# Modulation in quarters, tokens turned by a diagonal product, and a rebuilt path from row sums to routing in a one-layer mixture-of-experts kernel

## What is computed

```python
mod = silu(c) @ w_mod + b_mod            # shift, scale, gate of both halves of the layer
u   = rmsnorm(x, g1) * (1 + scale1) + shift1      # latent tokens; context tokens likewise with c_ctx
xr  = u @ w_in[:, :1024]                 # first projection, both token sets
h   = forward and backward gated recurrence over conv(xr)      # LRU, 4 heads x 2 directions
m   = sigmoid(.) * ((h * gelu(.)) @ w_rnn_proj) + sigmoid(.) * (pool_mixer(.) @ w_pool_proj)
x   = x + gate1 * rmsnorm(m @ w_out, g2)
v   = rmsnorm(x, g3) * (1 + scale2) + shift2
logits = v @ router_w + router_b         # 32 experts, the best 4 of each token, softmax over the 4
for e in range(32):
    z = v @ w1[e] + b1[e]                # 1024 -> 2048
    act = min(z0, 7) * sigmoid(1.702 * min(z0, 7)) * (clip(z1, -7, 7) + 1)
    out += comb[:, e] * (act @ w2[e] + b2[e])
x   = x + gate2 * rmsnorm(out, g4)
```

## Time and profile before

| | us |
|---|---|
| median of 3 runs | 1285.29 |
| lowest and highest run | 1284.62, 1285.57 |
| the profiled execution, device time | 1285.82 |
| its span, first to last instruction | 1283.8 |
| PE busy | 1234.7 (96%) |
| DVE, ACT, POOL busy | 361.8, 221.1, 43.9 |
| moved by DMA | 476.54 MB, mean 371 GB/s |

### The profile page before, as it was taken

How to read it: one execution, slowest core, us unless ns; L and a number is a source line. 1 busy time by engine, 2 the same in 40 slices (tenths; PEclk the granted TensorE clock), 3 DMA queues, 4 the chain that set the end, 5 groups by cost and what they waited for, 6 DMA issues and landing times.

```text
span 1283.8 us, 13953 instructions
## 1 busy us (share of the span) xinstructions
PE 1234.7 (96%) x5726; PEld 560.1 (44%) x5726; DVE 361.8 (28%) x641; ACT 221.1 (17%) x373; POOL 43.9 (3%) x90
## 2 busy tenths in 40 slices
PE   6999999999999999998999999999999899999997
PEld 4445688888443333332333333333333333333333
DVE  4567787342361112111111121112111111211113
ACT  3166631110231001010000110101110000110011
POOL 2000000240000000000000000000000000000000
PEclk9999999999999999999899999999999999999999
DMA  9732568997399999999999999999999999999995
GB/s 352 266 126 86 193 218 308 346 386 281 124 395 418 426 428 432 430 430 428 429 429 434 429 426 428 420 429 426 429 428 429 430 431 432 430 431 430 423 422 211
DMA packets 70350, 476.54 MB, mean 371 GB/s; under 512 B 6736, under 2 KB 38672, under 8 KB 48048
## 3 DMA queue, kind: packets, MB, share of 16 engines
q1 hardware_dynamic: 64320, 454.23, 85.8%
q0 software_dynamic: 3456, 21.24, 4.5%
q10 hardware_dynamic: 2512, 0.21, 0.1%
HBM read 474.60 MB, written 1.05 MB: 370 GB/s over the span
## 4 chain that ended last, share of the span: by engine, by line
PE 70%; DMA 20%; ACT 4%; DVE 4%; issue 1%; ACTq 0%; DVEq 0%; SPq 0%
PE bank L975 26%; DMA arena<-in_exp_w 20%; PE bank L992 13%; PE bank L814 11%; PE bank L1037 4%; PE bank L917 3%; PE bank L734 2%; PE bank L672 2%; PE bank L927 1%; PE bank L1084 1%; PE bank L750 1%; PE bank L700 1%; ACT arena L1195 1%; ACT arena L1189 1%; ACT arena L1197 1%
## 5 line engine op out<-in xcount | busy, mean ns | idle before, releaser
L975 PE MATMUL bank<-arena,temps 128*64 128x512 f32 x2112 | 473.0, 604 | 26.3 <-DMA arena<-in_exp_w 26.3
L975 PEld LDWEIGHTS bank<-arena,temps 128*64 128x64 f32 x2112 | 152.0, 139 | 328.6 <-issue 280.9
L992 PE MATMUL bank<-arena,vtokb 128*64 128x512 f32 x1024 | 226.8, 595 | 0.1
L1759 DVE TENSOR_SCALAR vtokb<-bank 128x512 f32<-128x512 f32 x33 | 22.8, 691 | 671.5 <-PE bank L975 671.5
L992 PEld LDWEIGHTS bank<-arena,vtokb 128*64 128x64 f32 x1024 | 70.6, 137 | 133.5 <-issue 128.0
L814 PE MATMUL bank<-arena 128*128 128x256 f32 x512 | 111.2, 379 | 0.0
L1304 ACT ACTIVATE vtokb<-vtokb 128x512 f32<-128x512 f32 x33 | 20.8, 629 | 504.5 <-DVE vtokb L1759 504.5
L814 PEld LDWEIGHTS bank<-arena 128*128 128x128 f32 x512 | 97.3, 190 | 14.9 <-issue 1.9
L1037 PE MATMUL bank<-vtokb,hot 64*128 64x512 f32 x256 | 65.4, 630 | 0.0
L750 PE MATMUL bank<-arena 128*128 128x512 f32 x128 | 56.3, 593 | 0.4 <-ACT arena L1190 0.4
L1319 ACT ACTIVATE vtokb<-bank 128x512 f32<-128x512 f32 x32 | 19.1, 598 | 204.1 <-PE bank L992 204.1
(11 more groups left out here) (286 smaller groups left out, 881.4 us busy)
## 6 DMA issues: line engine op xcount, KB each, us to landing
arena<-in_exp_w SPq DMA_DIRECT2D x115, 2048.0 KB, 22.8
arena<-in_exp_w SPq DMA_DIRECT2D x36, 4096.0 KB, 31.5
arena<-in_w_in SPq DMA_DIRECT2D x20, 1024.0 KB, 6.6
arena<-in_w_mod POOLq DMA_DIRECT2D x16, 1024.0 KB, 7.7
arena<-in_w_mod SPq DMA_DIRECT2D x16, 512.0 KB, 11.3
arena<-in_exp_w SPq DMA_DIRECT2D x6, 1024.0 KB, 22.0
arena<-in_w_pool_proj SPq DMA_DIRECT2D x4, 1024.0 KB, 14.1
arena<-in_w_rnn_proj SPq DMA_DIRECT2D x4, 1024.0 KB, 10.3
```

The lines of the kernel that those rows point to most:

```text
L975: done = mm(psum[4 + q][h * SLOTS:(h + 1) * SLOTS, :], xg[:, kx // 4, kx % 4, :], w1_at[s][:, r, o:o + HALF], start=False, stop=(k == KT - 1))
L992: last = mm(psum[6][h * SLOTS:(h + 1) * SLOTS, :], actT[:, c, r, :], w2_at[s][:, r, h * HALF:(h + 1) * HALF], start=(c == 0 and r == 0), s ...
L1759: v.tensor_scalar(glu, psum[4][:, :], LIMIT, None, ALU.min).then_inc(glu_ready, 1)
```

## The change

- *Tokens.* DVE no longer scales the tokens. It scales four copies of the identity by the tokens' inverse roots (`scaler`, 128x128), and PE multiplies each block of tokens with the diagonal: an ordinary product with 128 columns in place of a transpose.
- *Modulation.* `w_mod` comes in four quarters of 256 channels, two transfers of four rows for each operand (1 KB pieces instead of 2 KB). `mod_columns(g)` gives each channel block k a column group of its own (k mod 4) and 512 columns; the four partial sums are added by `turn_mod(g)`, which multiplies the copied rows with `fold`, a matrix of two columns. The first projection runs in quarters: for g = 0 to 2 all four j with k = 2g and 2g+1, with the next quarter's `mod_columns` ahead of j = 2 and its `turn_mod` inside j = 3; then j = 0 to 3 with k = 6 and 7. The first gates wait for all four quarters.
- *Row sums.* Two jobs in place of six. Each writes up to four sums side by side in column groups of 32, without the copy to all partitions; ACT copies them once and issues 24 transfers of 32x512 values that spread them. DVE makes the rows after the second pool projection has been read, not before the first.
- *Second token block.* Half of the scale product is made ahead (`scaled_parts`), the transposes start from that, DVE takes over one copy, the values are made in two halves behind the routing. `fill` products and the sums of the last gate's row (`sum_g2`) stand elsewhere.
- *Routing.* The mask comes from a replace-and-compare of the four best instead of indices and one-hot; the weights are made from all 32 exponentials.
- *Table and last chunks.* The table is turned ahead of the last part of item 0's first map. The last item's chunk 2 is loaded in two parts, chunk 3 in two instead of three.

```diff
-                    v.tensor_scalar(xin[:, t, :], xin[:, t, :], stat[:, 8 + t:9 + t], None, ALU.mult).then_inc(tok_scaled, 1)
+                    v.tensor_scalar(scaler[t], ident[:, :], stat[:, 8 + t:9 + t], None, ALU.mult).then_inc(tok_scaled, 1)
...
-                        last = nc.tensor.transpose(b[:, j * P:(j + 1) * P], xin[:, t, k * P:(k + 1) * P], ident[:, :])
+                        last = mm(b[:, j * P:(j + 1) * P], xin[:, t, k * P:(k + 1) * P], scaler[t], start=True, stop=True)
...
             def mod_columns(g):
...
-                    for q in range(2):
-                        for w in range(2):
-                            c = 32 * (2 * q + w)
...
-                            last = mm(psum[2 * g][c:c + 32, 0:256], sT[:, 32 * k:32 * k + 32], cols_q,
-                                      start=(k == 0), stop=(k == KT - 1))
...
+                    c = 32 * (k % 4)
+                    last = mm(psum[g % 2 * 2][c:c + 32, :], sT[:, 32 * k:32 * k + 32], modw[g][:, k, :, :],
+                              start=(k < 4), stop=(k >= 4))
...
             def turn_mod(g):
...
-                for j in range(2):
-                    last = nc.tensor.transpose(psum[2 * g + 1][:, j * P:(j + 1) * P], modrow[g][:, j * P:(j + 1) * P], ident[:, :])
+                for n in range(4):
+                    last = mm(psum[g % 2 * 2 + 1][:, 2 * n:2 * n + 2], modrow[g][:, n * P:(n + 1) * P], fold[:, :], start=True, stop=True)
...
+                    for g in range(3):
+                        for j in range(4):
+                            if j == 2:
+                                mod_columns(g + 1)
+                            if j == 3:
+                                xr_rows(j, 2 * g)
+                                turn_mod(g + 1)
+                            else:
+                                xr_rows(j, 2 * g)
+                            last = xr_rows(j, 2 * g + 1)
...
-                    end_job(mm(b[:, :], ones[:, :], acc[n // 4][:, n % 4 * HALF:(n % 4 + 1) * HALF], start=True, stop=True))
+                    for q in range(2 * len(ACC_ROWS[n])):
+                        last = mm(b[32 * q:32 * q + 32, :], ones[:, 0:32], acc[n][:, q * HALF:(q + 1) * HALF], start=True, stop=True)
...
+                        for to in range(0, P, 32):
+                            act.dma_start(row[g][to:to + 32, half * HALF:(half + 1) * HALF],
+                                          rowsum[n][p:p + 32, :]).then_inc(sums_landed, 16)
...
                 elif kind == "rk":
-                    fill(b, FILL[2] - 1)
                     sum_g2(1)
+                    fill(b, 2)
...
-                link(v.max_index(ixu[:, 8 * t:8 * t + 8], mx[:, t, :], lg[:, t, :]))
...
+                link(v.match_replace(lgr[:, t, :], mx[:, t, :], lg[:, t, :], NEVER))
+                v.tensor_tensor(mask[:, t, :], lgr[:, t, :], lg[:, t, :], ALU.not_equal).then_inc(mask_ready, 1)
```

More of the change, by code:

```diff
@@ L32 @@
 MORE = 16
-FILL = (3, 1, 2)
+NEVER = 3.0e38
 CPI = 6
@@ L85, in front_plan @@
     plan += [("pw", g, "A") for g in range(4)]
-    plan += [("rs", n, "A") for n in range(6)]
+    plan += [("rs", n, "A") for n in range(2)]
     plan += [("pp", c, "V") for c in range(4)]
@@ L758, in _ @@
                     mod_columns(0)
+                    pe.wait_ge(consts_ready, 2)
+                    fill(psum[3], 1)
                     turn_mod(0)
-                    fill(psum[3], 1)
+                    fill(psum[3], 1, 256)
                     arrive("xr", 0)
@@ L850, in _ @@
                         k = 4 * q + j
-                        last = nc.tensor.transpose(b[:, j * P:(j + 1) * P], mG[:, t, k * P:(k + 1) * P], ident[:, :])
+                        last = nc.tensor.transpose(b[:, j * P:(j + 1) * P], mG[:, 0, k * P:(k + 1) * P], ident[:, :])
                     end_job(last)
@@ L959, in first_map @@
                         pe.wait_ge(xg_ready, 2)
+                    if first and c == 3:
+                        turn_table()
                     s = slot_of(i, c)
@@ L1153, in _ @@
             a.activation(lamw[:, 16:32], lamw[:, 0:16], ACT.Exp, scale=-1.0).then_inc(lam_exp, 1)
-            for g in range(2):
+            for g in range(4):
                 act.wait_ge(mod_ready, g + 1)
@@ L1157, in _ @@
                 act.wait_ge(read_dve, read_at[number["xt", 3]][1])
-                for k in range(4 * g + 1, 4 * g + 4, 2):
+                for k in (2 * g + 1,):
                     for s in range(2):
@@ L1228, in _ @@
                 ins.then_inc(read_act, 1)
-            for n in range(6):
+            for n in range(2):
                 b = job_of("rs", n)
-                r = row[ACC_ROWS[n // 4][n % 4 // 2]]
-                a.activation(r[:, n % 2 * HALF:(n % 2 + 1) * HALF], b[:, :], ACT.Copy).then_inc(read_act, 1)
+                used = 64 * len(ACC_ROWS[n])
+                a.activation(rowsum[n][0:used, :], b[0:used, :], ACT.Copy).then_inc(read_act, 1)
+                act.wait_ge(read_act, read_at[number["rs", n]][1])
+                for m, g in enumerate(ACC_ROWS[n]):
+                    for half in range(2):
+                        p = 32 * (2 * m + half)
+                        for to in range(0, P, 32):
+                            act.dma_start(row[g][to:to + 32, half * HALF:(half + 1) * HALF],
+                                          rowsum[n][p:p + 32, :]).then_inc(sums_landed, 16)
             a.activation(stat[:, 16:18], ones[:, 0:2], ACT.Sqrt).then_inc(act_warm, 1)
@@ L1425, in take_mod @@
                 dve.wait_ge(read_dve, read_at[number["xt", 3]][1])
-                for k in range(4 * g, 4 * g + 4, 2):
+                for k in (2 * g,):
                     for s in range(2):
@@ L1615, in tokens_of, with residual, variance_of_sum @@
                 link(v.reciprocal(stat[:, 18 + t:19 + t], stat[:, 16 + t:17 + t]))
+            def residual(t, h):
                 dve.wait_ge(xres_landed, 16)
+                r = slice(h * HALF, (h + 1) * HALF)
+                v.scalar_tensor_tensor(x1[:, t, r], mG[:, t, r], stat[:, 18 + t:19 + t], x1[:, t, r],
+                                       ALU.mult, ALU.add).then_inc(x1_ready, 1)
+            def variance_of_sum(t):
+                dve.wait_ge(ssq3_ready, 2 * t + 2)
+                s0, s1 = (small[:, 68 + 2 * t + q:69 + 2 * t + q] for q in range(2))
+                link(v.tensor_tensor(stat[:, 20 + t:21 + t], s0, s1, ALU.add))
+                v.tensor_scalar(stat[:, 22 + t:23 + t], stat[:, 20 + t:21 + t], 1.0 / D, EPS, ALU.mult, ALU.add).then_inc(var3, 1)
@@ L1673, in _ @@
             for t in range(TT):
[L1674 to L1680 removed]
+                ins = v.scalar_tensor_tensor(comb_v[:, t, :], ex[:, t, :], small[:, 48 + t:49 + t], mask[:, t, :], ALU.mult, ALU.mult)
+            ins.then_inc(comb_ready, 1)
             dve.wait_ge(comb_ready, 1)
```

272 lines of the change are left out of this document (148 added, 124 removed).

## The result

The changed kernel takes 1300.35 us (median of 4, 1298.41 to 1301.97) against 1285.43 for the kernel before on the same chip: ratio 1.0116, 95% interval 1.0103 to 1.0129. That is 14.9 us slower, where 2.2 were forecast, and outside the range. The profiled execution took 1299.69 us with a span of 1298.0, 14.2 more than before; I work with that difference.

The account below looks back on a forecast made before the run. PE was taken to bound the kernel up to its last output projection, then the expert weight stream. 7.0 - 3.4 - 1.1 - 0.3 = +2.2 us gave 1287.5 against 1285.29, range 1283.5 to 1291.0.

Parts of the forecast that it names:

- cost 0: Spreading the row sums by 24 transfers: cover of 3 to 7 us before PE's small product, so no added time.
- second part: Row sums: two jobs of 0.86 us replace 5.14 us on PE, minus 3.4 us, with nothing waiting in their place.
- What bounds the kernel: PE up to its last output projection at 347.5 us, each microsecond moving the end by one; then the expert weight stream.
- Start of the projection: First projection after tokens and first modulation quarter: starts at 23.3 us, 1.3 earlier than before (bounds 22.5 and 24.5).
- The factor of the diagonal product: Token blocks: a diagonal product costs twice a transpose, 0.22 against 0.13 us at the fast clock, not the skill's factor.
- Three rounds and the turns: First projection in quarters, from start to end: 37.1 us, including three gaps of 0.5 us.
- The wait for convolution 1: Ahead of the first gates: convolution 1 is done 2.7 us after the projection, gates start at 63.1, 7.0 later.
- Row sums on PE: Row-sum products on PE: two jobs in place of twelve records, minus 3.4 us.
- The spread transfers: ACT's 24 row-sum transfers: issued by about 274 us, spread finished likely at 299, needed at 306; cost 0.
- Routing and last chunks: After the output projection: routing minus 1.1 us, expert 0 starting 0.3 earlier; last item's chunks minus 0.3.
- The rivals: Quarters pay: 1281.3, 12%; routing pays in full: 1285.1, 13%; spread sums late: 1292, 12%; diagonal costs four transposes: 1294, 3%.
- spread sums come late: Ahead of the last rp product: slow landings make PE wait until 311 instead of 306, plus 4.5, 1292; chance 12%.

## Why the prediction was wrong, step by step

The step that failed is the term "cost 0" of the second part: "nothing waits in their place", and the spread "off the path". PE did wait, for weights of another queue, and that made 8.1 of the 12.7 us by which the forecast missed. The start makes 2.3 more (9.3 for 7.0), routing and last chunks 1.4, the row sums 0.4; 0.5 are left over.

- **What bounds the kernel.** Right for the expert part, and right that each microsecond up to `wo_done` counts once. This is where the omission lies: "up to there PE is the bound" was read from PE's busy time alone. From 256 to 300 us the transfer engines are as full as in the expert part, and no row of that stretch's transfer share stood in the argument. Two of these rows of before (columns as in the earlier trace rows) show it, a transfer share of 1.10 and 1.09:

```profile
256.00:262.00 6.00, 6.00 (x18) 3.03 (x17) 0.00 (x0) 3.86 (x8) 5.85 (x3) 1.00 1.10 412
...
292.00:296.00 4.00, 4.00 (x20) 3.54 (x19) 0.00 (x0) 0.00 (x0) 0.00 (x0) 1.00 1.09 393
```

- **Start of the projection.** Forecast 23.3, measured 24.08. The blocks end at 18.96 (18.2). The first 32 records took 6.05 us; at 0.12 and 0.217 a record the rise to the fast level comes at about 13.5 by my estimate (13.3), and a fast record of 128 columns takes 0.12 (3.84 / 32), not 0.11. In the eight kernels with the diagonal products these 32 records took 5.18 to 6.54 us. So where the rise comes differs from one execution to the next, and the start's time with it by over a microsecond; that the forecast came so near is partly luck.
- **The factor of the diagonal product.** Two records of 0.12 make 0.24 us a block at the fast level against 0.13 for a transpose: 1.85, near the two that I took. The factor of four that the Trainium skill gives ("TensorE: Matmul & The Clock Gate", Terms) isn't seen here, and the diagonals as a whole cost 1.0 us by themselves and 1.9 on top of the quarters.
- **Three rounds and the turns.** Forecast 37.1, measured 38.2: each round 10.3 to 10.4 instead of 10.07. The 16 records of a round stand in three pieces and take 7.4 us instead of 6.85; the gaps were 0.3 each, smaller than the 0.5 forecast.
- **The wait for convolution 1.** Forecast 2.7, measured 2.60, and its chain is borne out. What stood behind it in the profiled execution was missing: gates at half the clock, 1.7 us, from a cause that the runs leave open. Together the start was forecast at 7.0 and came to 10.4 in the profiled execution, 9.3 in the runs with it alone.
- **Row sums on PE.** Forecast -3.4, measured -3.3; and -3.0 end to end in the run that gives the transfers room.
- **The spread transfers.** "Cost 0" was true for the path that I priced: DVE had the correction ready at 311, and PE would have been there at 317. Untrue for the one I didn't: the weights of `rp` on another queue, over the same engines. The text did say "DMA is busy at that time, and 1.5 MB more are moved", and took it only as a risk for the spread's own landing. From rows of before it could have been priced: 1.5 MB at 430 GB/s is 3.7 us at least (5.8 in truth), and 3.3 us less time up to the need. Against this stood the slack of the second chunk: issued at 275.8, there by 291.6 if it took the longest of the four landing times of before (15.8), wanted at 296.3, so 4.7. That leaves 2.3 us of wait by the lower price and 4.4 by the measured one; 5.2 were measured. The products behind the wait, slow at half the clock (2.6), come on top.
- **Routing and last chunks.** Forecast -1.4, measured 0. Expert 0 came 0.5 us earlier, a little more than priced (0.3). That the stream would use it is not borne out.
- **The rivals.** None of them was the case. The mechanism of "spread sums come late" (small transfers that land late beside bulk) is real, and decides as soon as the loads are moved (7.4, 8.8 and 14.4 us).

The sum after the runs: start 9.3, row sums -3.0, weights 8.1 (the whole change less the run with the loads moved), the rest 0, makes 14.4 of 14.9.

## What to carry to other kernels

Price an added transfer against every deadline that shares its engines, not only against its own. A step that becomes shorter on the bounding engine also brings forward each load that is wanted behind it, so read the transfer share of that stretch first; and where the engines are full, look for loads whose need is far off and move them behind the urgent ones, small transfers above all. The best version here (1281.5) keeps the old start, takes the new row sums, and issues 4 MB of expert weights some 40 us later.

## What the runs showed of the hardware

- An idle time of 2.60 us on PE ahead of the same gates was followed by half the clock in five kernels (16 records in 8.77 to 8.80 us) and by full clock in the one with quarters alone (7.10), where PE's work ahead of it stood 0.8 to 1.2 us earlier. 1.40 us in another kernel, just as early, were followed by full clock. What decides isn't shown.
- Copies within the SBUF of 32 rows by 2 KB ran at 269 GB/s per share of engine time, weights beside them at 339 (estimates from the queues' shares).
- SP's own time to issue the same four transfers of `w_out` grew with the work in front of them: 2.42 us with the expert chunks moved away, 4.00 before, 13.67 with the spread transfers.
- Eight transfers of 0.5 KB took up to 32 us from their first issue until DVE could read them beside expert weights (288.24 to 320.20), 23 in another kernel (300.8 to 324.2), and at most 8.8 us where SP held the weights back (287.97 to 296.73).
